# One loop body for all sixteen experts, with the last expert's first two weight blocks parked in two places through the whole stage

## What is computed

```python
def expert_choice_ffn(h, w_router, w1, w3, w2):
    cap = EC_CAPACITY * L // N_EXPERTS            # 64 latent, 16 context tokens for each expert
    aff = jax.nn.softmax((h @ w_router).astype(jnp.float32), axis=-1)
    gate, idx = lax.top_k(aff.transpose(0, 2, 1), cap)
    xs = jax.vmap(lambda hb, ib: hb[ib])(h, idx)
    a = jnp.einsum('becd,edf->becf', xs, w1)
    b = jnp.einsum('becd,edf->becf', xs, w3)
    y = jnp.einsum('becf,efd->becd', jax.nn.silu(a) * b, w2) * gate[..., None].astype(h.dtype)
    # y is added back to the rows idx of the result
```

## Time and profile before

| | us |
|---|---|
| median of 3 runs | 2695.71 (2691.11 to 2699.36) |
| the profiled execution, its own time | 2696.3 |
| its span, first to last instruction | 2694.5 |
| PE busy | 2520.7 (94%) |
| expert stage of layer 0, first to last expert matmul | 865.6 to 1338.3 |
| expert stage of layer 1 | 2186.9 to 2661.3 |

### The profile page before, as it was taken

One profiled execution on the slowest core, in us unless ns is written; L12 is line 12 of the kernel. 1 busy time (PEld: TensorE's weight loads), 2 busy tenths in 40 slices (PEclk: granted clock), 3 DMA queues, 4 the chain that ended last, 5 costly groups with the idle time before them and its releaser, 6 DMA issues.

```text
span 2694.5 us, 79955 instructions
## 1 busy us (share of the span) xinstructions
PE 2520.7 (94%) x31456; PEld 1918.2 (71%) x31456; DVE 1164.1 (43%) x2031; ACT 814.8 (30%) x3454; POOL 961.5 (36%) x2976
## 2 busy tenths in 40 slices
PE   6999999999997999999889999999999969999995
PEld 3555676666755899888746566766666559988885
DVE  3998534555426111111278874345644341111114
ACT  3112223434214343333021132334331143433320
POOL 2374223232201255445535632133221014554444
PEclk9999999999999999999999999999999979999998
DMA  8332311112336899999723322111242249999993
GB/s 329 114 146 94 113 60 50 67 63 103 148 125 256 327 427 428 427 427 427 331 102 125 132 95 92 61 66 53 105 167 74 113 159 404 427 427 427 428 427 148
DMA packets 45134, 572.39 MB, mean 212 GB/s; under 512 B 5248, under 2 KB 7424, under 8 KB 9600
## 3 DMA queue, kind: packets, MB, share of 16 engines
q1 hardware_dynamic: 42336, 553.67, 50.7%
q10 hardware_dynamic: 2592, 16.38, 1.5%
HBM read 561.11 MB, written 8.91 MB: 212 GB/s over the span
## 4 chain that ended last, share of the span: by engine, by line
PE 67%; DMA 20%; DVE 10%; issue 2%; ACT 1%; DVEq 0%; POOL 0%; POOLq 0%; ACTq 0%
PE ps L511 50%; DMA ring<-in_w_exp 18%; PE ps L678 6%; DVE region_b L1707 5%; PE ps L933 3%; DMA ring<-in_w_last 2%; PE ps L899 1%; PE ps L882 1%; PE ps L870 1%; PE ps L1043 1%; DVE region_r L1996 1%; DVE rstd L1621 0%; DVE region_r L1995 0%; DVE region_r L1999 0%; PE ps L785 0%
## 5 line engine op out<-in xcount | busy, mean ns | idle before, releaser
L2321 POOL TENSOR_TENSOR region_m<-region_m,region_r 128x8 f32 x2416 | 424.1, 217 | 542.8 <-DVE region_r L2036 489.3
L511 PE MATMUL ps<-hT,ring 128*128 128x320 f32 (+2 forms) x1440 | 429.0, 440 | 8.4 <-ACT hT L1221 8.2
L2329 ACT ACTIVATE region_b<-hT 128x8 f32 x2400 | 290.6, 204 | 270.4 <-DVE region_r L2049 158.9
L511 PEld LDWEIGHTS ps<-hT,ring 128*128 128x128 f32 x1440 | 256.2, 191 | 145.0 <-issue 65.7
L511 PE MATMUL ps<-region_r,ring 128*64 128x80 f32 x7812 | 287.3, 233 | 22.2 <-DMA ring<-in_w_exp 19.3
L511 PEld LDWEIGHTS ps<-region_r,ring 128*64 128x64 f32 x7812 | 278.3, 137 | 28.9 <-DMA ring<-in_w_exp 25.8
L1707 DVE SCALAR_TENSOR_TENSOR region_b<-region_b,params 128x655 f32<-128x655 f32 x240 | 277.6, 1157 | 8.5
L511 PE MATMUL ps<-region_b,ring 128*128 128x320 f32 (+1 forms) x812 | 191.7, 373 | 0.5 <-DMA ring<-in_w_last 0.5
L511 PE MATMUL ps<-region_r,spare 128*64 128x80 f32 x4032 | 152.6, 237 | 27.9 <-DVE region_r L2331 18.1
L2167 POOL TENSOR_TENSOR params<-ring 128x512 f32<-128x512 f32 x32 | 41.9, 1310 | 372.2 <-DMA ring<-in_w_pair 370.7
L511 PEld LDWEIGHTS ps<-region_r,spare 128*64 128x64 f32 x4032 | 147.7, 140 | 32.0 <-DVE region_r L2331 18.6
(11 more groups left out here) (291 smaller groups left out, 3778.8 us busy)
## 6 DMA issues: line engine op xcount, KB each, us to landing
region_b<-in_w_exp SPq DMA_DIRECT2D x60, 2048.0 KB, 25.2
ring<-in_w_exp SPq DMA_DIRECT2D x60, 2048.0 KB, 25.3
ring<-in_w_mix SPq DMA_DIRECT2D x39, 2048.0 KB, 8.1
region_x<-in_w_exp SPq DMA_DIRECT2D x30, 2048.0 KB, 25.2
spare<-in_w_exp SPq DMA_DIRECT2D x30, 2048.0 KB, 25.3
ring<-in_w_pair SPq DMA_DIRECT2D x32, 1536.0 KB, 6.4
ring<-in_w_ada SPq DMA_DIRECT2D x4, 2048.0 KB, 10.3
x_store<-region_m ACTq DMA_DIRECT2D x2, 2560.0 KB, 10.6
```

What stands on the lines that cost most here:

```text
L511: ins = pe.matmul(*args, **kw)
L2321: last = eng.tensor_tensor(x[:, :, token], x[:, :, token], y_gated[e % 2][:, :, c:c + 1], ALU.add)
L2329: last = eng.activation(into[:, :, c:c + 1], h[:, :, token], ACT.Copy)
```

## The change

The ring for experts' blocks is now `EXP_SLOTS` = (4, 1, 5, 2, 3, 0). Places 7 and 6 hold blocks 90 and 91, the last expert's first a and b block (`KEPT`). Blocks are now numbered by expert: a, b, a, b, y, y. PE's loop body is one whole expert (four up blocks, one gate matmul, two down blocks) and serves all sixteen. It is an inner loop inside an outer loop of two turns. The first outer turn runs experts 1 to 15 (counted from 1) and then, after the inner loop, the two blocks that are parked; the second runs the body once for expert 16, with an `If` that jumps over its first two blocks. Four blocks (128 records each) that stood ahead of the loop, and two behind it, are gone; two stand now inside the outer loop. The gates are laid and spread for one expert at a time. `y` has two banks. DVE's help for the last expert but one is gone. The two rounds for context tokens stand ahead of the last latent round. In layer 0 the modulation blocks 0 to 2 are loaded early in places 7, 6 and 3, and the experts' blocks behind them.

```diff
-ADA_SLOTS = (0, 1, 2, 0)
-FIRST_SLOTS = (7, 3, 6, 0)
-LOOP_SLOTS = (4, 1, 5, 2, 7, 3)
+ADA_SLOTS = (7, 6, 3, 0)
+EXP_SLOTS = (4, 1, 5, 2, 3, 0)
+KEPT_FIRST = EXP_BLOCKS * (NE - 1)
+KEPT = {KEPT_FIRST: 7, KEPT_FIRST + 1: 6}
...
@@ SP, between the last weight pairs and after them
                     if (name, p) == ("pair", 11):
-                        load_expert(0)
+                        load_next_ada(0) if l == 0 else load_expert(KEPT_FIRST)
...
                         sp.wait_ge(kv_stored, 2 * 16 * (l + 1))
-                        load_expert(2)
+                        load_next_ada(1) if l == 0 else load_expert(KEPT_FIRST + 1)
...
                         need("br_step", 56)
-                        load_expert(1)
+                        load_next_ada(2) if l == 0 else load_expert(4)
...
                 need("br_read", 32)
...
+                load_expert(0)
+                load_next_ada(3) if l == 0 else load_expert(5)
+                load_expert(1)
+                need("ctx_out_done", 2)
+                load_expert(2)
+                load_expert(3)
                 if l == 0:
...
+                    load_expert(4)
+                    load_expert(5)
+                    for n in KEPT:
+                        load_expert(n)
+                for n in range(EXP_BLOCKS, EXP_BLOCKS * NE):
+                    if n not in KEPT:
+                        load_expert(n)
@@ PE
-                up_blocks(0, 0, 0, True)
-                spread_gates()
-                up_blocks(1, 2, 0, False)
-                with pe.Fori(1, NE) as e:
-                    need("xs_ready", e)
-                    up_blocks(2 * e, FIRST_BLOCKS, e - 1, False)
-                    down_block(2 * e, FIRST_BLOCKS + 2, e - 1)
-                    up_blocks(2 * e + 1, FIRST_BLOCKS + 3, e - 1, False)
-                    down_block(2 * e + 1, FIRST_BLOCKS + 5, e - 1)
-                for b in range(LAST_BLOCKS):
-                    need("act_ready", HALVES)
-                    expert_block(FIRST_BLOCKS + LOOP_BLOCKS + b, 0, last_banks[b], act_last, "y_done")
+                with pe.Fori(0, 2) as last:
+                    with pe.Fori(last * (NE - 1) + 1, last + NE) as e:
+                        with pe.If(NE - e):
+                            need("xs_ready", e)
+                            up_half(e, 0, 0, e - 1)
+                        up_half(e, 2, 1, e - 1)
+                        spread_gates(e)
+                        for half in range(2):
+                            down_block(4 + half, e, half)
+                    with pe.If(1 - last):
+                        need("xs_ready", NE)
+                        up_half(NE, KEPT_FIRST, 0, 0)
...
+                def down_block(n, e, half):
+
+                    w = weights(EXP_AT[l] + n, e - 1)
+                    need("y_copied", 2 * e - 1 + half)
+                    for part in range(2):
+                        if part and not half:
+                            need("b_used", 2 * e + 1)
+                        for m in range(4):
+                            for k in range(part * KC // 2, (part + 1) * KC // 2):
+                                ins = expert_step(w, y_banks[half], act, m, k, (m, k) == (0, 0))
+                    ins.then_inc(S["y_done"], 1)
@@ ACT
+                need("index_ready", 8)
+                take_slots(nc, sc, mybir.EngineType.Activation, index, 0, h, xs, CAPL, CAPL + 8)
                 need("index_ready", 9)
-                take_slots(nc, sc, mybir.EngineType.Activation, index, 0, h, xs, CAPL, CAPL + 5).then_inc(S["xs_first"], 1)
+                take_slots(nc, sc, mybir.EngineType.Activation, index, 0, h, xs, CAPL - 8, CAPL - 5).then_inc(S["xs_first"], 1)
...
+                        next_slots(e + 1, 0, PARKED)
                     silu(2 * e)
@@ DVE
-                take_slots(nc, v, mybir.EngineType.DVE, index, 0, h, xs, CAPL + 5, CAPL + 11).then_inc(S["xs_first"], 1)
+                take_slots(nc, v, mybir.EngineType.DVE, index, 0, h, xs, CAPL - 3, CAPL).then_inc(S["xs_first"], 1)
...
+                for e in range(NE):
+                    for half in range(2):
+                        i = 2 * e + half
+                        need("b_done", i + 1)
+                        need("sil_ready", i + 2)
+                        v.tensor_tensor(flat(act)[:, half * HC:(half + 1) * HC], b_ps, sil[half], ALU.mult)\
+                            .then_inc(S["b_used"], 1)
+                    if e < NE - 1:
+                        need("xs_parked", e + 1)
+                        v.tensor_copy(flat(xs), flat(xs_next)).then_inc(S["xs_ready"], 1)
...
+                    copy_y(2 * e)
+                    copy_y(2 * e + 1)
+                    if e < NE - 1:
+                        lay_gates(e + 1)
```

More of the change, by code:

```diff
@@ L44 @@
 CAP = CAPL + CAPC
-HELPED = 48
+PARKED = 48
 HALVES = 2 * NE
@@ L153 @@
     for _n in range(EXP_BLOCKS * NE):
-        take(FIRST_SLOTS[_n] if _n < FIRST_BLOCKS else LOOP_SLOTS[(_n - FIRST_BLOCKS) % EXP_BLOCKS], expert=(_l, _n))
+        take(KEPT.get(_n, EXP_SLOTS[_n % EXP_BLOCKS]), expert=(_l, _n))
 def tile_count(phase, m):
@@ L608, in ada_turn @@
                         last = pe.transpose(ps[:, 1, m * P:(m + 1) * P], row[:, n % 2, m * P:(m + 1) * P], ident)
+                        if m == 0 and pending:
+                            last.then_inc(slot_used[pending.pop(0)], 1)
                     last.then_inc(S["ada_turned"], 1)
@@ L1127, in layer, with spread_gates, expert_step, up_block @@
                 turn_logits(2)
-                next_ada(("turn", 1), ("rows", 2))
+                next_ada(("turn", 1), ("rows", 2), ("turn", 2), ("rows", 3), ("turn", 3))
                 turn_affinities(2)
[L1130 to L1144, removed]
+                def spread_gates(e):
+                    need("gates_laid", e)
+                    pe.matmul(gate_bank, ones[0:NE, :], gates_laid, start=True, stop=True).then_inc(S["gates_wide"], 1)
+                def expert_step(w, ps, moving, m, k, start):
+                    for at in range(0, P, WCOLS):
+                        ins = pe.matmul(
+                            ps[at:at + WCOLS, m * CAP:(m + 1) * CAP],
+                            w[:, k, m * P + at:m * P + at + WCOLS], moving[:, k, :],
+                            start=start, stop=k == KC - 1, tile_position=(0, at), skip_group_check=True)
+                    return ins
+                def up_block(n, turns, ps, done):
                     w = weights(EXP_AT[l] + n, turns)
@@ L1148, in expert_block @@
                         for k in range(KC):
[L1149 to L1154, removed]
@@ L1155, in expert_block @@
-                    ins.then_inc(S[done], 1)
[L1157 to L1170, removed]
@@ new lines, in layer, with up_half @@
+                assert not pending
+                need("xs_first", 3)
+                if l + 1 < LAYERS:
+                    pe.wait_ge(S["ada_part_in"], ADA_BLOCKS * (l + 1) + ADA_EARLY[l + 1])
+                def up_half(e, n, half, turns):
+                    need("sil_ready", 2 * e - 1 + half)
+                    up_block(n, turns, a_ps, "a_done")
+                    need("b_used", 2 * e - 1 + half)
+                    up_block(n + 1, turns, b_ps, "b_done")
+                with pe.Fori(0, 2) as last:
[10 more added lines that the diff above has]
+                        up_half(NE, KEPT_FIRST, 0, 0)
@@ L2027, in copy_y @@
                         need("y_added", e - 1)
[L2028 to L2031 removed]
+                    v.tensor_tensor(y_gated[e % 2][:, rows, :], y_banks[half].rearrange("p (k c) -> p k c", k=4),
                                     token_gates[:, rows, :], ALU.mult).then_inc(S["y_copied"], 1)
[L2033 removed]
@@ L2040, in layer @@
-                for i in range(HALVES):
-                    e, half = divmod(i, 2)
-                    need("b_done", i + 1)
-                    need("sil_ready", i + 1)
-                    if half == 0:
-                        into = sil[0] if e < NE - 1 else flat(act_last)[:, 0:HC]
-                        inc(v.tensor_tensor(into, PS[0][:, 1, 0:HC], sil[0], ALU.mult), "b_used")
-                    elif e < NE - 1:
+                v.sem_inc(S["xs_ready"], 1)
+                v.sem_inc(S["b_used"], 1)
@@ L2048, in layer @@
+                v.sem_inc(S["y_copied"], 2)
+                for e in range(NE):
+                    for half in range(2):
[5 more added lines that the diff above has]
+                    if e < NE - 1:
                         need("xs_parked", e + 1)
```

143 lines of the change are left out of this document (48 added, 95 removed).

## The result

The changed kernel takes **2833.27 us** (median of 4, 2826.40 to 2833.62), the kernel before, beside it on the same chip, 2696.38 us (4 runs, 2691.11 to 2699.36): ratio 1.0504 [1.0481, 1.0527]. The prediction was 2720, 24 us more; it is 137 us more.

A forecast was written before the change was run, and what follows sets the result against it. Transfers at 5.035 us a block were taken to bound the stages, PE their ends. Block 89's landing plus 33.3 and 16.7 us gave +12.4 and +11.5, so 2696.3 + 23.9 = 2720.2, forecast 2720, range 2692 to 2729.

The forecast's parts named there:

- Then the new loop closes at once and PE runs at 4.43 us: Expert stage's start: after six new blocks PE runs 4.43 us a block; block 15 lands 2.6 (layer 0), 3.6 us (layer 1) earlier.
- the loop's code is kept: Expert loop before the change: no code packet moves in some 13 turns of the six-block loop, from 935 to 1330 us.
- All code is kept: Rival: no refetch at the outer jump, each stage ends 33.3 us behind block 89; 2686 us, chance 0.11.
- the others: Rivals: only the header missing, 6 us a layer, 2698 (0.32); loads slower than thought, 2726 or 2704 (0.12).
- The outer jump: Jump back to expert 16: all its code is fetched again, none of it covered, 16.7 us a layer; refetch chance 0.45.
- my 6 and 5: Outer jump: 6 us for the header's packet, 5 us for the packet to which the `If` jumps.
- The 3.7 us: Outer jump: the packet after the `If`'s is asked for only then, with a quarter block left to run; 3.7 us.
- 82 to 84: Whole kernel: code packets on the page if the outer jump's code is fetched again; about 72 if all is kept.
- The start of the stream: Stage's start: block 11 issued at 898.5 in layer 0, block 89 landing at 1300.7 and 2622.8, 2.6 and 3.6 us earlier.
- third rival: First turn's code packets hold the load stream back, so 2.6 and 3.6 us are lost: 2726 or 2704; chance 0.12.
- The parked pair: Stage's end: blocks 90 and 91 already there, so 33.3 us behind block 89's landing, 1.6 less than before.
- covered edits: Expert stages: gate matmul, `If`, POOL's adds and ACT's columns fit in free time; failed cover costs its overhang 15 times a layer.

The follow-up runs named there:

- three kernels with both loops held: Changed kernel with two, eight or 32 idle PE instructions ahead of layer 1's expert loop: 2709.95, 2712.80 and 2714.3 us.
- first try on the kernel before: Kernel before the change with 73 idle PE instructions ahead of layer 0's expert loop and 171 more ahead of layer 1's: 2701.38 us.
- written-out version: Changed kernel without outer loop and `If`: fifteen experts looped, expert 16 written out, 20 idle PE instructions ahead of layer 1's loop; 2691.86 us.
- shifted kernel: Changed kernel with 32 idle PE instructions ahead of layer 1's expert loop: 2714.3 us, ratio to before 1.0064.
- half-loaded kernel: Changed kernel, unpadded, all expert blocks but the first six and the parked two loading only half their columns: 2799.97 us in one run.

## Why the prediction was wrong

**The step that failed:** "Then the new loop closes at once and PE runs at 4.43 us", for layer 1. It rested on the earlier trace rows, "the loop's code is kept", read as a property of a six-block loop. The runs show it for a loop that touches seven packets. In layer 0 the step held; in layer 1 the loop touched eight, lost its code at every second jump back, and the stage took 599.4 us instead of 479.5 with two idle instructions. The kernel with two idle instructions shows the size of this one step: 2709.95 instead of 2833.27. Without it the forecast would have been 6 to 10 us too high (2709.95 to 2714.3 in the three kernels with both loops held) and in its range. None of my rivals had it; "All code is kept" and the others all took the inner loop for held. The risk could be seen beforehand, in the program's length in packets and the count of instructions ahead of each loop; which way it falls could hardly be, as the first try on the kernel before shows: the same count missed a window of 12 instructions.

**The outer jump** was priced at 16.7 us a layer. It costs 10.9 and 10.6 beyond the written-out version. In layer 0 of the changed kernel it is one stop of 9.04 us: no matmul stands between the header and the place to which the `If` jumps, so it stands for my 6 and 5 together. The 3.7 us are not there, and one small stop of 0.91 us is. The next two blocks take 1.6 us more behind the stop (10.65 against 9.01), which the sum did not have. That the blocks are fetched again and not kept was right, and I had too few packets: 91 with both loops held, where I had 82 to 84. With the new blocks' own stops in, the whole end was predicted at 50.0 us behind block 89 and took 44.5 (layer 0), 43.4 with the loop held (layer 1).

**The start of the stream.** Block 11 was to be issued at 898.5 in layer 0, 33.3 us behind the stage's start, as before the change. SP's issue of it in the changed kernel

```profile
902.36 0.33 SPq L425 DMA_DIRECT2D ring<-in_w_exp  x1
```

and in the written-out version, whose first turn is the same code,

```profile
898.60 0.33 SPq L425 DMA_DIRECT2D ring<-in_w_exp  x1
```

lie 38.1 and 37.1 us behind their stages' starts (864.26 and 861.55). Six new blocks under the first transfers cost 3.8 to 4.8 us more than I gave them (stops of 1.46, 1.83, 0.97 and 2.45 us in the changed kernel). The issue was 3.9 us late against the forecast, and block 89 with it, at 1305.09 instead of 1300.7. This is the third rival, and in layer 0 it happened, with more than the 2.6 us that it had. In layer 1 block 89 started 436.5 us behind the stage's start in the shifted kernel, and 439.6 before the change: 3.1 us gained, 3.6 predicted. In layer 0 the late stream (+4.4) and the cheaper end (-5.5) cancel, which is why its end was hit to 1.1 us: two errors, not one right number.

**The parked pair and the covered edits.** The pair's worth is as above. The gates, POOL's 80 adds and ACT's columns stayed covered: layer 0's steady part runs at the rate of the transfers (427 GB/s), and the written-out version with the pair loaded late has all of them and is level with before (1.0003). The `If` stands only in the kernels with the outer loop, whose excess over before, 13.6 to 20.0 us, is less than their two outer jumps.

**Code kept.** The Trainium skill (Runtime: NRT & Kernel Launch, Instruction fetch mechanics) gives PE 128 KiB in blocks of 16 KiB, from which eight packets is an estimate. The runs agree: a loop on seven packets stays (no code packet in twelve turns), one on eight does not (79 in the stage). I had read it as a bound for the outer loop alone. The rule in the same section of the Trainium skill, of a window of two pages for a taken branch, is contradicted by each held turn, whose jump costs 0.16 to 0.38 us.

**Still open:** why with full queues only every second turn fetches (nine packets in two turns), and with half of the bytes every one (38 packets in the four turns from 2199.4 to 2351 us, so nine or ten in each). Every second is not a fixed rule either: in the kernel with 80 idle instructions the jumps at 1075.00 and 1122.13, one turn apart, both stop (13.00 and 11.43 us), and nine packets move behind the first. And whether the limit is eight packets or has to do with a jump to the last instructions of a packet: I moved the loop, but did not build loops of other lengths, and none began 10 or 20 instructions ahead of an edge.

**A version that beats both** was not found. The written-out kernel is level with before (0.9991 [0.9980, 1.0002]).

## What to carry to other kernels

A PE loop whose code nearly fills what is kept (6.05 to 6.09 packets here) is fast or slow by the place of its first instruction. So when an edit adds or removes code ahead of such a loop, count the instructions up to it, and see how many packets it may touch; the count alone can miss by a few instructions, but the code packets in the profile (80 before, 154 after) tell at once whether a loop is held. If it is not, a few idle instructions ahead of it are the first thing to try. A long stop by "issue" at the jump back, here at every second one, is its mark.

A comparison of two versions that differ in code length can measure this accident and not the idea: here the idea with its outer loop costs 14 to 20 us, written out nothing, and the accident 87 to 120 us a stage.

## What the hardware showed that I had not expected

- Two instructions decide 123 us (2833.27 to 2709.95).
- A stop for code is 8.1 us with half of the bytes, 11.4 to 13.5 with all of them in mid-stage, and 7.7 to 10.1 at the outer jump (11.0 with half of the bytes), where the transfers are nearly done (36 GB/s in the 9.04 us).
- Behind such a stop the granted clock is 0.50 and then 0.71 for some 8 us; the next 379 records take 16.18 us. In the half-loaded kernel this costs 2.2 to 2.5 us of each turn.
- The stream of 2 MB transfers stops with PE: 0 to 6 GB/s from 2274 to 2282 us, because every load waits for a block that PE ends.
